# Low halves of weights by an accumulating DMA, and small tasks in other slots, in a two-block kernel

## The chip, the cores and the metric

One core of a Trainium2 chip runs the whole program. The metric is the device time of one execution in microseconds, from start to end of the program on that core; lower is better. All data is float32, and the products must be close to those of float32.

## The reference

Two transformer-like blocks, one after the other, on 256 tokens with 2048 features.

```python
# first block
h = rms(x) ; proj = h @ w_in                       # 8 parts of 1024 columns
y_rec = hgrn2(q, f_fwd, f_bwd, i, gate)            # gated linear recurrence in both directions, 8 heads
y_conv = b * conv3(c * h_conv)                     # short convolution, width 3
x = x + concat(y_rec, y_conv) @ w_out
x = x + (silu(g) * u) @ w_down                     # g, u = rms(x) @ w_gate_up, 5632 each
x = rms(x)
# second block
sh1, sc1, gt1, sh2, sc2, gt2 = split(silu(c) @ w_ada + b_ada)
h = rms(x) * (1 + sc1) + sh1 ; proj = h @ w_in_2
y_a = latent attention with rope, 8 heads ; y_b = stick-breaking attention, 8 heads
x = x + gt1 * ((sig(gl_a) * (y_a @ w_mla) + sig(gl_b) * (y_b @ w_sb)) @ w_out_2)
h2 = rms(x) * (1 + sc2) + sh2
x = x + gt2 * ((silu(gate) * up) @ w_ffn_out)      # gate, up = h2 @ w_ffn_in, 5632 each
```

## The kernel before, in words

All weights are read once from HBM, in units of 512 rows by 512 columns (1 MB, `raw`, four buffers, loaded by SyncE at L2009). A unit is worked off in two chunks (`hf` 0 and 1) of 256 rows. TensorE has a fast form of float32 (fp32r) that keeps only the high bits, so each product is made of three: every operand is split into a high half, which fp32r holds exactly, and a low half, the rest. ScalarE makes the high half of a chunk (`whi`, L865, in `cast(c)`), VectorE the low half (`wlo = raw - whi`, L1257, in `low(c)`), and TensorE then adds high x high, low x high and high x low into one accumulator (L834 to L836, in `products(v)`). There are four such buffers (HL = 4). A chunk is 12 products of 512 columns (two feature tiles, two halves m of the tokens, three terms).

The order of the work is written out in advance by `Plan`. A visit is one chunk on TensorE; slot s of an engine's program is its small tasks (`side_work(s)`) followed, on TensorE, by the products of visit s. On ScalarE slot s then casts the chunk that is three visits ahead (AHEAD), as soon as its buffer is free, which is when the visit before s has ended; on VectorE the lows of slot s - 1 stand first in slot s, then the tiles of the `ada` product, which VectorE computes alone (L1684), then the small tasks. SyncE loads unit u as soon as the last chunk of unit u - 4 has its low half. GpSimd does only the 20 small powers (x to the -0.5, L1933).

A block is a set of 512 columns of one matrix; `block_side(b, t)` holds what each engine does in slot t after the block's last visit. The blocks that the change touches:

- `h` (L1341, VectorE): the convolution in four parts, t = 3 to 6, two per half of the tokens; its result is used by block `b` at t = 2, eight slots after `h` ends.
- `hgrn(g, u)`: the recurrence of head group g as tasks u, one per slot, from slot H0 on. u = 0 to 2: Qx and KC (L1607, L1610), the latter used by TensorE at u = 3 (L633). Levels follow. u = 29, 30: outputs `hout` on TensorE. u = 30, 31: their squares summed on VectorE (L1634), mean, then the power on GpSimd. u = 32: scaling (L1641), u = 33: times the gate (L1647). u = 34, 35: TensorE turns the result (L553 is every turn's line), ScalarE writes its high half (L879), and at u = 35, 36 VectorE its low half (L1271).
- `latent` (t = 3: turns and high halves; t = 4: low halves).
- `gate_tiles` (L1720 to L1728): four times from slot GT0 on, every second slot; in the next slot TensorE spreads them over partitions (L733, L734) and ScalarE copies them to `gtB`. `gated_add` (L1537, L1545) uses gtB at the end of each `out2` block.
- `boundary(w, k)`: the two norms between blocks (w = 0, 1). There the order is skewed: the last four chunks of the old block are visited for m = 0 (k = 0 to 3), then for m = 1 (k = 4 to 7), then the first four chunks of the new one for m = 0 (k = 8 to 11) and m = 1 (k = 12 to 15), each visit six products. VectorE at k = 4: `add(0)`, `scale(0)`, `y0(0)` (L1808); TensorE turns the normed rows in pieces p (`norm_first(w, 0, p)`, amid the visits k = 6 to 9); ScalarE scales and shifts a turned piece (`shifted`, L1195), for p = 2 VectorE does it (L1846); VectorE splits it into halves (`piece`, L1815, L1817), which the visits from k = 8 on need; then the same for m = 1 (`add(1)` is L1528 and L1530 at w = 0).
- The start: 26 warm-up products (WARM, L841) before the first real one.

In the second ffn (blocks `fgate`, `fup` with arg (2, j)) the columns are done in two parts, j = 0 to 5 and 6 to 10, each followed by its four `fdown` blocks. At the end of each fgate block ScalarE does two sigmoids (L933) ahead of its cast. Units of `w_ada` are woven in; the last of them comes before the second part.

Of the kernel before, what the change touches and what calls it, by code (L numbers as in the profile page):

```python
# [28 lines left out]
WARM = 26  # L29
# [82 lines left out]
class Plan:  # L112


    def __init__(self, rows):
        self.blocks = plan_blocks()
        self.at = {(b.kind,) + b.arg: b for b in self.blocks}
        self.units, self.chunks, self.ada_unit = [], [], {}
        todo = [(j, g) for j in range(24) for g in range(4)]
        since = -4  # L120
        every_of = {"out": 4, "fgate": 2, "fup": 2, "fdown": 2}
        for b in self.blocks:
            if b.kind == "fgate" and b.arg == (2, 0):
                since = -4
            ng = rows[b.name] // NBLOCKS[b.name]
            for gi, g in enumerate(b.groups):
                u = len(self.units)
                self.units.append((b.name, b.nb * ng + g))
                for hf in range(1 if b.kind == "kpe" else 2):
                    self.chunks.append((b, 2 * gi + hf, u, hf))  # L130
                since += 1
                every = 4 if b.lhs == "h1" else every_of.get(b.kind)
                if b.kind == "fdown" and b.arg in ((1, 1, 2), (1, 1, 3)):
                    every = None
                late = b.kind[0] == "f" and b.arg[0] == 2
# [151 lines left out]
def two_block_kernel(nc, a, out):  # L287
    ctx = ExitStack()
    with ctx:
# [158 lines left out]

        def raw_here(u):
# [5 lines left out]
        sem_side = [sem(f"s_side{i}") for i in range(4)]  # L455
        sem_raw = [sem(f"s_raw{i}") for i in range(RAW)]
# [64 lines left out]
        GT0 = {2: pl.end("sb", 3) + 2, 5: pl.ada_done[23] + 2}  # L521
# [29 lines left out]
        def tensor_program(e):  # L551
# [18 lines left out]
            def block_side(b, t):  # L570
# [22 lines left out]
                elif kind == "latent" and t == 3:  # L593
# [25 lines left out]
            def hgrn(g, u):  # L619
# [34 lines left out]
                elif u in (34, 35):  # L654
                    p2 = u - 34
# [43 lines left out]
            def side_work(s):  # L699
# [103 lines left out]
            def products(v):  # L803
# [3 lines left out]
                if ms[0] == 0:  # L807
                    e.wait_ge(*on("dve_lo", c, 0))
# [39 lines left out]
        def scalar_program(e):  # L848
            def cast(c):
# [15 lines left out]
                e.copy(whi[i][:, :, :], raw[u % RAW][:, 2 * hf:2 * hf + 2, :]).then_inc(*ev("act_hi", c, 0))  # L865
# [16 lines left out]
            def block_side(b, t):  # L882
# [84 lines left out]
                elif kind == "latent" and t == 3:  # L967
# [76 lines left out]
            def hgrn(g, u):  # L1044
# [21 lines left out]
                elif u in (34, 35):  # L1066
                    scaled_high(mH, ("hturn", g, u - 34), 4 * g + 2 * (u - 34), "hgrn_norm_w")
# [97 lines left out]
            def boundary(w, k):  # L1165
# [42 lines left out]
                elif k == 7:  # L1208
                    shifted((0, 0), AUX[0], 0, P)
                    shifted((0, 1), AUX[1], 2, P)  # L1210
                elif k == 8:
                    squares(1)
                    shifted((0, 3), AUX[3], 6, P)
# [30 lines left out]
        def vector_program(e):  # L1244
            def low(c):
# [3 lines left out]
                if c == 0:  # L1249
                    for k in range(2):  # L1250
# [3 lines left out]
                        feature(1 + k)  # L1254
                    return
# [55 lines left out]
            def block_side(b, t):  # L1311
# [29 lines left out]
                elif kind == "h" and 3 <= t < 7:  # L1341
                    g, m, half = b.arg[0], (t - 3) // 2, (t - 3) % 2
# [94 lines left out]
                elif kind == "latent" and t == 4:  # L1437
# [161 lines left out]
            def hgrn(g, u):  # L1599
                lev = hlev(u) if u >= 6 else None  # L1600
                if u in (0, 1):
                    if u == 0:
# [3 lines left out]
                        e.wait_ge(*on("dve_gates", g, 0, 5))  # L1606
                    e.tensor_tensor(Qx[:, u, :], qT[:, :], TA[:, 1024 * u:1024 * u + 1024], ALU.mult).then_inc(  # L1607
                        *ev("dve_hgrn", g, "q", u))
                elif u == 2:
                    e.tensor_tensor(KC[:, :], Kx[:, 0, :], Kx[:, 1, :], ALU.add).then_inc(*ev("dve_hgrn", g, "kc"))  # L1610
# [20 lines left out]
                elif u in (30, 31):  # L1631
# [3 lines left out]
                    if m:  # L1635
                        e.wait_ge(*on("dve_hgrn", g, "ss", 1))
                        mean(("hgrn", g), b_o[g], 8, P)
                elif u == 32:
                    e.wait_ge(*on("pool_pow", "hgrn", g))
                    for m in range(2):  # L1640
                        e.tensor_tensor(v4(T[m]), v4(side("hout", g, m)),  # L1641
# [7 lines left out]
                elif u in (35, 36):  # L1649
                    scaled_low(mH, mL, ("hturn", g, u - 35), 4 * g + 2 * (u - 35), "hgrn_norm_w")  # L1650
# [126 lines left out]
            def boundary(w, k):  # L1777
# [62 lines left out]
                elif k == 8:  # L1840
                    add(1)
# [7 lines left out]
                    piece(0, 2)  # L1849
                    scale(1)  # L1850
                    piece(0, 3)
# [77 lines left out]
        def gpsimd_program(e):  # L1929
# [7 lines left out]
            for g in range(2):  # L1937
                power(b_s[g], b_o[g], 8, "hgrn", g)
# [12 lines left out]
            for m in range(2):  # L1951
                power(b_r5 + m, b_r5 + m, 1, "norm", 1, m)


        def sync_program(e):
# [34 lines left out]
            for u, (name, k) in enumerate(pl.units):  # L1990
# [10 lines left out]
                if u >= RAW:  # L2001
# [3 lines left out]
                    else:  # L2005
                        e.wait_ge(*on("dve_lo", pl.last_chunk[u - RAW], 0))
# [124 lines left out]
```

## Time and profile before

| what | value |
|---|---|
| median of 2 runs | 2611.93 us (2611.53 to 2612.33) |
| the profiled execution | 2611.4 us |
| its span, first to last instruction | 2609.6 us |
| granted TensorE clock, mean | 0.998 |
| read from HBM | 578.36 MB, 222 GB/s over the span |

Times in rows are microseconds from the span's start unless marked ns. PE is TensorE's products, PEld its weight loads, DVE VectorE, ACT ScalarE, POOL GpSimd, SP SyncE. L12 is line 12 of the kernel before. Matmuls are pipelined: a record of 0.39 us is followed by the next start 0.23 us later. A releaser (<-) is what ended an idle time.

### The profile page before, as it was taken

The page shows a single profiled execution, that of the slowest core. Times are in us where ns is not written, and L with a number is a line of the kernel's source. Part 1 is how long each engine was busy: PE and PEld are TensorE (multiplying, and loading weights), DVE is VectorE, ACT ScalarE, POOL GpSimd, SP SyncE. Part 2 cuts the span into 40 slices and gives each one's busy share as a digit, 9 for nine tenths or more (in the row PEclk, how much of TensorE's full clock was granted, in tenths as well). Part 3 has the DMA queues.
Part 4 walks back from the last instruction along what each step waited for, and adds up shares of the span by engine and source line. Part 5 has one row for each costly group of instructions (what it writes and reads, how often), then busy time and mean ns, then how long its engine had stood idle before and what let it go on. Part 6 is the DMA issues. An engine that isn't in the chain of part 4 may idle for free.

```text
span 2609.6 us, 29547 instructions
## 1 busy us (share of the span) xinstructions
PE 2591.0 (99%) x11900; PEld 2152.0 (82%) x11900; DVE 1757.9 (67%) x2156; ACT 1198.8 (46%) x1465; POOL 26.4 (1%) x25
## 2 busy tenths in 40 slices
PE   9999999999999999999999999999999999999999
PEld 8887887888888888888788888888788888888887
DVE  6777687787777778886565455466677755555554
ACT  6444544444443344445655454444544443344443
POOL 0000000000000000000000000000000000000000
PEclk9999999999999999999999999999999999999999
DMA  8655656688788887776455445555477755555554
GB/s 323 220 191 201 221 194 220 239 298 288 276 290 288 289 285 281 282 285 234 156 173 175 145 162 180 193 190 179 163 280 283 274 177 194 193 193 194 179 193 144
DMA packets 82632, 582.37 MB, mean 223 GB/s; under 512 B 9409, under 2 KB 9793, under 8 KB 12609
## 3 DMA queue, kind: packets, MB, share of 16 engines
q1 hardware_dynamic: 82352, 580.38, 63.3%
q8 instruction: 94, 1.54, 0.2%
q14 instruction: 42, 0.34, 0.0%
q10 hardware_dynamic: 144, 0.12, 0.0%
HBM read 578.36 MB, written 2.10 MB: 222 GB/s over the span
## 4 chain that ended last, share of the span: by engine, by line
PE 96%; DVE 3%; ACT 1%; issue 1%; DMA 0%; POOL 0%; ACTq 0%; DVEq 0%
PE bank L834 30%; PE bank L836 30%; PE bank L835 30%; PE bank L553 2%; PE bank L633 1%; DVE wlo L1257 1%; DVE adacc L1684 0%; PE bank L671 0%; PE bank L682 0%; PE bank L683 0%; ACT whi L865 0%; DVE Qx L1607 0%; DVE tmp L1355 0%; PE bank L652 0%; PE bank L641 0%
## 5 line engine op out<-in xcount | busy, mean ns | idle before, releaser
L1257 DVE TENSOR_TENSOR wlo<-raw,whi 128x1024 fp32r<-128x1024 f32 x886 | 1082.0, 1223 | 740.2 <-ACT whi L865 731.7
L865 ACT CAST whi<-raw 128x1024 fp32r<-128x1024 f32 x886 | 932.9, 1054 | 1017.4 <-PE bank L836 1007.3
L834 PE MATMUL bank<-whi,hH 128*128 128x512 f32 x2528 | 997.8, 395 | 0.5 <-DVE wlo L1252 0.5
L836 PE MATMUL bank<-whi,hL 128*128 128x512 f32 x2528 | 985.9, 390 | 0.0
L835 PE MATMUL bank<-wlo,hH 128*128 128x512 f32 x2528 | 985.0, 390 | 0.0
L836 PEld LDWEIGHTS bank<-whi,hL 128*128 128x128 f32 x2528 | 474.9, 188 | 99.9
L834 PEld LDWEIGHTS bank<-whi,hH 128*128 128x128 f32 x2528 | 475.5, 188 | 97.3 <-issue 0.9
L835 PEld LDWEIGHTS bank<-wlo,hH 128*128 128x128 f32 x2528 | 475.7, 188 | 95.9
L834 PE MATMUL bank<-whi,aH 128*128 128x512 f32 x704 | 274.5, 390 | 0.0
L1684 DVE SCALAR_TENSOR_TENSOR adacc<-raw,stat,adacc 128x512 f32<-128x512 f32 x360 | 269.6, 749 | 6.8
L836 PE MATMUL bank<-whi,aL 128*128 128x512 f32 x704 | 274.0, 389 | 0.0
L835 PE MATMUL bank<-wlo,aH 128*128 128x512 f32 x704 | 273.9, 389 | 0.0
L834 PEld LDWEIGHTS bank<-whi,aH 128*128 128x128 f32 x704 | 132.1, 188 | 27.3
L835 PEld LDWEIGHTS bank<-wlo,aH 128*128 128x128 f32 x704 | 132.2, 188 | 27.3
L836 PEld LDWEIGHTS bank<-whi,aL 128*128 128x128 f32 x704 | 132.1, 188 | 27.3
L553 PE MATMUL bank<-ident,tmp 128*128 128x128 f32 x530 | 75.0, 274 | 8.1 <-DVE tmp L1647 6.5
L553 PEld LDWEIGHTS bank<-ident,tmp 128*128 128x128 f32 x530 | 63.4, 141 | 23.6 <-DVE tmp L1647 7.3
L834 PE MATMUL bank<-whi,mH 128*128 128x512 f32 x128 | 51.3, 401 | 0.0
L836 PE MATMUL bank<-whi,mL 128*128 128x512 f32 x128 | 50.7, 396 | 0.0
L835 PE MATMUL bank<-wlo,mH 128*128 128x512 f32 x128 | 50.4, 394 | 0.0
L940 ACT CAST aH<-bank 128x512 fp32r<-128x512 f32 x44 | 23.6, 590 | 45.6 <-PE bank L553 45.6
L1933 POOL TENSOR_TENSOR stat<-stat 128x4 f32<-128x4 f32 (+3 forms) x20 | 24.4, 1231 | 1834.0 <-DVE stat L1277 1073.6
(295 smaller groups left out, 1421.8 us busy)
## 6 DMA issues: line engine op xcount, KB each, us to landing
raw<-in_w_gu_dram SPq DMA_DIRECT2D x176, 1024.0 KB, 4.9
raw<-in_w_ada_dram SPq DMA_DIRECT2D x96, 1024.0 KB, 4.8
raw<-in_w_down_dram SPq DMA_DIRECT2D x88, 1024.0 KB, 4.8
raw<-in_w_in_dram SPq DMA_DIRECT2D x62, 1024.0 KB, 4.8
raw<-in_w_in2b_dram SPq DMA_DIRECT2D x56, 1024.0 KB, 4.8
raw<-in_w_out_dram SPq DMA_DIRECT2D x32, 1024.0 KB, 4.8
raw<-in_w_in2a_dram SPq DMA_DIRECT2D x8, 1024.0 KB, 5.0
raw<-in_w_mla_dram SPq DMA_DIRECT2D x8, 1024.0 KB, 4.8
```

What stands on the lines that cost most here:

```text
L553: return e.transpose(o, i, ident[0:n, 0:n])
L633: ins = e.matmul(o[:, P * hd:P * hd + P], KC[:, base:base + P], qq, start=True, stop=True)
L834: e.matmul(o, xh[:, kt, sl], wh[:, i, :], start=k == 0, stop=False)
L835: e.matmul(o, xh[:, kt, sl], wl[:, i, :], start=False, stop=False)
L836: ins = e.matmul(o, xl[:, kt, sl], wh[:, i, :], start=False, stop=k == n - 1)
L865: e.copy(whi[i][:, :, :], raw[u % RAW][:, 2 * hf:2 * hf + 2, :]).then_inc(*ev("act_hi", c, 0))
L940: e.copy(aH[:, k0:k0 + 4, P * m:P * m + P], v4(side(b.index, m))).then_inc(*ev("act_half", b.index, m))
L1257: e.tensor_tensor(wlo[i][:, :, :], raw[u % RAW][:, 2 * hf:2 * hf + 2, :], f(whi[i][:, :, :]), ALU.subtract).then_inc(*ev("dve_lo", c, 0))
L1684: ins = e.scalar_tensor_tensor(d, src, col, d, ALU.mult, ALU.add)
L1933: e.tensor_tensor(sc(o, n), sc(i, n), sc(b_half, n), ALU.pow).then_inc(*ev("pool_pow", *key))
```

## The change

Ten edits.

1. `pl.added`: of the blocks fgate and fup (2, j) with j >= 6, every second unit, those whose last chunk is number 3 or 7 of its block (so chunks 2, 3, 6 and 7 of each of the ten blocks). For their chunks VectorE makes no low half. ScalarE writes, after the high half, minus the raw data rounded to fp32r (which is minus the high half) into `wlo`, and GpSimd issues a DMA that adds the raw data, read again from HBM, onto it. TensorE waits for that DMA (`added_low`), and SyncE's next load into the raw buffer waits for the negative copy instead of the low half.
2. WARM 26 to 30.
3. GT0 of part 2 one slot later.
4. `latent` turns and high halves at t = 4, low halves at t = 5.
5. hgrn's turns at u = 35, 36 and their low halves at 36, 37.
6. hgrn's KC at u = 0, the two Qx at u = 1 and 2.
7. hgrn's mean and power for each half m by itself.
8. The convolution at t = 3, 4 (first half of the tokens) and 8, 9 (second).
9. `norm_first(w, 0, p)`: p = 0, 1 before the visit k = 7, p = 2, 3 amid it, in place of one in each of k = 6 to 9.
10. At k = 7 ScalarE also shifts p = 3, and VectorE does its share of p = 2 and all four pieces; at k = 8 add(1), scale(1), y0(1) follow.

```diff
+        self.added = {u for u, c in self.last_chunk.items()
+                      if self.chunks[c][0].kind in ("fgate", "fup") and self.chunks[c][0].arg[0] == 2
+                      and self.chunks[c][0].arg[1] >= 6 and self.chunks[c][1] in (3, 7)}
...
-        GT0 = {2: pl.end("sb", 3) + 2, 5: pl.ada_done[23] + 2}
+        GT0 = {2: pl.end("sb", 3) + 3, 5: pl.ada_done[23] + 2}
...
-                elif u in (34, 35):
-                    p2 = u - 34
+                elif u in (35, 36):
+                    p2 = u - 35
...
+                for w, v0 in enumerate(SK):
+                    if s == v0 + 7:
+                        norm_first(w, 0, 0)
+                        norm_first(w, 0, 1)
...
-                    if 6 <= k <= 9:
-                        norm_first(w, 0, k - 6)
+                    if k == 7:
+                        norm_first(w, 0, 2)
+                        norm_first(w, 0, 3)
...
-                    e.wait_ge(*on("dve_lo", c, 0))
+                    e.wait_ge(*(added_low(c) if u in pl.added else on("dve_lo", c, 0)))
...
-                e.copy(whi[i][:, :, :], raw[u % RAW][:, 2 * hf:2 * hf + 2, :]).then_inc(*ev("act_hi", c, 0))
+                src = raw[u % RAW][:, 2 * hf:2 * hf + 2, :]
+                e.copy(whi[i][:, :, :], src).then_inc(*ev("act_hi", c, 0))
+                if u in pl.added:
+                    e.activation(wlo[i][:, :, :], src, ACT.Copy, bias=0.0, scale=-1.0).then_inc(*ev("act_neg", c))
...
+                if u in pl.added:
                     return
...
-                elif kind == "h" and 3 <= t < 7:
-                    g, m, half = b.arg[0], (t - 3) // 2, (t - 3) % 2
+                elif kind == "h" and t in (3, 4, 8, 9):
+                    g, m, half = b.arg[0], int(t >= 8), (t - 3) % 5
...
+            for c in added_chunks:
+                b, ci, u, hf = pl.chunks[c]
+                name, k = pl.units[u]
+                e.wait_ge(*on("act_neg", c))
+                e.dma_start(wlo[pl.buf[c]][:, :, :].rearrange("p a b -> p (a b)"),
+                            a[name][k][:, 1024 * hf:1024 * hf + 1024], accum_op=ALU.add).then_inc(
+                    sem_add[pl.buf[c] % HL], 16)
...
-                        e.wait_ge(*on("dve_lo", pl.last_chunk[u - RAW], 0))
+                        if u - RAW in pl.added:
+                            e.wait_ge(*on("act_neg", pl.last_chunk[u - RAW]))
+                        else:
+                            e.wait_ge(*on("dve_lo", pl.last_chunk[u - RAW], 0))
```

## Rows read from the trace of the kernel before

**Rows 1.** The page: busy time, share of the span, instructions.

```profile
PE 2591.0 (99%) x11900; PEld 2152.0 (82%) x11900; DVE 1757.9 (67%) x2156; ACT 1198.8 (46%) x1465; POOL 26.4 (1%) x25
```

**Rows 2.** Waits of TensorE, whole span: us in total, times, longest.

```profile
PE bank L553 <- DVE tmp L1647: 6.5, 2, 3.2
PE bank L834 <- DVE hL L1817: 1.7, 2, 0.8
PE bank L733 <- DVE tmpr L1728: 1.6, 1, 1.6
...
PE bank L553 <- DVE tmp L1808: 1.1, 2, 0.7
...
PE bank L633 <- DVE KC L1610: 0.4, 2, 0.2
```

**Rows 3.** Windows: PE, PEld, DVE, ACT, POOL busy; clock, DMA share, GB/s.

```profile
211.70:215.10 3.40, 2.71 (x9) 2.33 (x10) 1.77 (x3) 1.55 (x3) 0.00 (x0) 0.50 0.86 280
...
1803.00:1806.00 3.00, 1.40 (x7) 0.83 (x6) 2.96 (x6) 0.87 (x3) 0.00 (x0) 1.00 0.00 0
```

**Rows 4.** Timeline, 202 to 213: start, us, engine, line, [idle before].

```profile
202.45 0.47 DVE L1352 TENSOR_SCALAR tmp<-U,vec 128x128 f32<-128x128 f32 x2
202.84 1.13 DVE L1355 SCALAR_TENSOR_TENSOR tmp<-U,vec,tmp 128x128 f32<-128x128 f32 x4
...
211.05 1.28 DVE L1647 TENSOR_TENSOR tmp<-tmp,Gg 128x512 f32<-128x512 f32 x2
...
204.86 2.56 POOL L1933 TENSOR_TENSOR stat<-stat 128x8 f32<-128x8 f32 x1 [157.50 <-DVE stat L1277]
...
212.39 1.12 PE L553 MATMUL bank<-ident,tmp 128*128 128x128 f32 x4 [3.24 <-DVE tmp L1647]
```

**Rows 5.** Timeline of VectorE: the gated add ahead of the fourth gate tiles.

```profile
1800.80 0.69 DVE L1537 TENSOR_TENSOR tmp<-bank,gtB 128x512 f32<-128x512 f32 x1
```

**Rows 6.** Timeline of the first norm boundary: VectorE, then one turn on TensorE.

```profile
1242.50 0.29 DVE L1815 CAST hH<-aux 128x256 fp32r<-128x256 f32 x1 [1.37 <-ACT aux L1195]
1242.83 0.43 DVE L1817 TENSOR_TENSOR hL<-aux,hH 128x256 fp32r<-128x256 f32 x1
...
1244.78 0.68 DVE L1528 TENSOR_TENSOR tmp<-x,bank 128x512 f32<-128x512 f32 x1
...
1246.11 0.72 DVE L1846 TENSOR_SCALAR adacc<-bank,stat,adaF 128x128 f32<-128x128 f32 x2
...
1248.76 0.48 DVE L1808 TENSOR_SCALAR tmp<-x,stat 128x512 f32<-128x512 f32 x1
...
1249.91 0.38 PE L553 MATMUL bank<-ident,tmp 128*128 128x128 f32 x2
```

**Rows 7.** The start: timeline of TensorE, then a window (columns as in rows 3).

```profile
1.08 5.81 PE L841 MATMUL bank<-ones_r 128*128 128x128 f32 x26 [1.08 <-DVE ones_r L1908]
...
7.44 0.80 PE L834 MATMUL bank<-whi,hH 128*128 128x512 f32 x1 [0.55 <-DVE wlo L1252]
...
7.50:10.20 2.70, 2.70 (x7) 2.14 (x8) 2.52 (x5) 2.64 (x6) 0.00 (x0) 1.00 0.98 301
```

**Rows 8.** Timeline in the second part: ScalarE's casts, one product of TensorE.

```profile
2386.42 1.05 ACT L865 CAST whi<-raw 128x1024 fp32r<-128x1024 f32 x1
2388.17 1.05 ACT L865 CAST whi<-raw 128x1024 fp32r<-128x1024 f32 x1 [0.70 <-PE bank L836]
2390.89 1.05 ACT L865 CAST whi<-raw 128x1024 fp32r<-128x1024 f32 x1 [1.67 <-PE bank L836]
...
2387.97 0.39 PE L834 MATMUL bank<-whi,hH 128*128 128x512 f32 x1
```

**Rows 9.** Windows of that part (columns as in rows 3); landing of L2009's loads.

```profile
2275.00:2497.00 222.00, 222.00 (x997) 184.10 (x996) 116.90 (x112) 93.87 (x99) 0.00 (x0) 1.00 0.56 191
...
2389.70:2393.10 3.40, 3.40 (x17) 2.81 (x16) 1.91 (x2) 1.05 (x1) 0.00 (x0) 1.00 0.91 308
...
DMA to landing us min/median/max: 4.6/4.8/6.2
```

More of the change, by code:

```diff
@@ L28 @@
 SPARE = 4
-WARM = 26
+WARM = 30
 LIFE = 14
@@ L447, in side_read, with added_low @@
             return sem_side[n % 4], n // 4 + 1
+        def added_low(c):
+            return sem_add[pl.buf[c] % HL], 16 * sum(1 for d in added_chunks if d <= c and pl.buf[d] == pl.buf[c])
         def raw_here(u):
@@ L455, in two_block_kernel @@
         sem_side = [sem(f"s_side{i}") for i in range(4)]
+        sem_add = [sem(f"s_add{i}") for i in range(HL)]
+        added_chunks = [c for c, ch in enumerate(pl.chunks) if ch[2] in pl.added]
         sem_raw = [sem(f"s_raw{i}") for i in range(RAW)]
@@ L592, in block_side @@
                         ins.then_inc(*ev("pe_turn", b.index, m))
-                elif kind == "latent" and t == 3:
+                elif kind == "latent" and t == 4:
                     for p2 in range(2):
@@ L966, in block_side @@
                             *ev("act_lat", b.index, m))
-                elif kind == "latent" and t == 3:
+                elif kind == "latent" and t == 4:
                     for p2 in range(2):
@@ L1065, in hgrn @@
                         *ev("act_sq", "hout", g, m))
-                elif u in (34, 35):
-                    scaled_high(mH, ("hturn", g, u - 34), 4 * g + 2 * (u - 34), "hgrn_norm_w")
+                elif u in (35, 36):
+                    scaled_high(mH, ("hturn", g, u - 35), 4 * g + 2 * (u - 35), "hgrn_norm_w")
             def mla_head(h, t):
@@ L1210, in boundary @@
                     shifted((0, 1), AUX[1], 2, P)
+                    shifted((0, 3), AUX[3], 6, P)
                 elif k == 8:
                     squares(1)
-                    shifted((0, 3), AUX[3], 6, P)
                     y1(1)
@@ L1254, in low @@
                         feature(1 + k)
+                    return
+                if u in pl.added:
                     return
@@ L1436, in block_side @@
                         *ev("dve_mean", "latent", i))
-                elif kind == "latent" and t == 4:
+                elif kind == "latent" and t == 5:
                     i = b.arg[0]
@@ L1600, in hgrn @@
                 lev = hlev(u) if u >= 6 else None
-                if u in (0, 1):
-                    if u == 0:
+                if u == 0:
+                    e.wait_ge(*on("dve_gates", g, 0, 5))
+                    e.tensor_tensor(KC[:, :], Kx[:, 0, :], Kx[:, 1, :], ALU.add).then_inc(*ev("dve_hgrn", g, "kc"))
+                elif u in (1, 2):
+                    z = u - 1
+                    if z == 0:
                         q = pl.at["q", g].index
@@ L1605, in hgrn @@
                         e.wait_ge(*side_read(q, 1))
[L1606 to L1610, printed above, removed]
+                    e.tensor_tensor(Qx[:, z, :], qT[:, :], TA[:, 1024 * z:1024 * z + 1024], ALU.mult).then_inc(
+                        *ev("dve_hgrn", g, "q", z))
                 elif lev is not None:
@@ L1634, in hgrn @@
                     e.tensor_reduce(sc(b_o[g] + 4 * m, 4), v4(T[m]), AX_X, ALU.add).then_inc(*ev("dve_hgrn", g, "ss", m))
-                    if m:
-                        e.wait_ge(*on("dve_hgrn", g, "ss", 1))
-                        mean(("hgrn", g), b_o[g], 8, P)
+                    e.wait_ge(*on("dve_hgrn", g, "ss", m))
+                    mean(("hgrn", g, m), b_o[g] + 4 * m, 4, P)
                 elif u == 32:
-                    e.wait_ge(*on("pool_pow", "hgrn", g))
                     for m in range(2):
+                        e.wait_ge(*on("pool_pow", "hgrn", g, m))
                         e.tensor_tensor(v4(T[m]), v4(side("hout", g, m)),
@@ L1648, in hgrn @@
                             *ev("dve_hgrn", g, "gated", m))
-                elif u in (35, 36):
-                    scaled_low(mH, mL, ("hturn", g, u - 35), 4 * g + 2 * (u - 35), "hgrn_norm_w")
+                elif u in (36, 37):
+                    scaled_low(mH, mL, ("hturn", g, u - 36), 4 * g + 2 * (u - 36), "hgrn_norm_w")
             def carry(g, lev, t4, z, half, tz, name):
@@ L1839, in boundary @@
                     piece(0, 1)
-                elif k == 8:
-                    add(1)
                     o = side("norm", w, 0, 2)
@@ L1849, in boundary @@
                     piece(0, 2)
+                    piece(0, 3)
+                elif k == 8:
+                    add(1)
                     scale(1)
-                    piece(0, 3)
                     y0(1)
@@ L1937, in gpsimd_program @@
             for g in range(2):
-                power(b_s[g], b_o[g], 8, "hgrn", g)
+                for m in range(2):
+                    power(b_s[g] + 4 * m, b_o[g] + 4 * m, 4, "hgrn", g, m)
             power(b_r2, b_r2, 2, "r2")
```

## Prediction

> **What bounds the kernel now.** I read the page first: TensorE is busy for 2591.0 of 2609.6 us, 99% of the span, while VectorE has 67% and GpSimd 1% [rows 1]. So no other engine's work has a price of its own; only what TensorE waits for, or the rate at which it runs, can change. That leaves 18.6 us of idle time. The waits of TensorE by line come second [rows 2]: two waits of 3.2 us for the hgrn groups' gated values, 1.6 us for the first gate tiles, and 1.7 + 1.1 us for norm pieces and L1808 at the two norm boundaries. The rest is smaller waits, the start and the end. Third, the stretches around the two long waits by windows: the granted clock is 0.50, the lower of its two levels (1.2 instead of 2.4 GHz), for 3.4 us after a gap of 3.24 us (there are two such gaps, alike; the first is shown); around the gap of 1.6 us it stays at 1.00 [rows 3]. At half rate 3.4 us of busy time give 1.7 us of work, so each long gap costs 3.2 + 1.7 = 4.9 us.
>
> **The change, part by part.**
>
> *hgrn tail (tasks u = 30 to 37).* Before, TensorE reaches the turn of u = 34 when its products end, 3.24 us before it can start it at 212.39. VectorE is late: the convolution stands in slot 31 (202.45 to 203.97, 1.5 us) and again in slot 32 ahead of the sum of squares, and of the scaling L1641, and L1647 ends at 212.33 [rows 4]. The change takes both parts out of these slots (to t = 8, 9), splits the power by m, and puts the turn one slot later. Of the 3.0 us of convolution that go, the casts that wlo waits for, which TensorE's own pace sets, give back some; the 1.5 us of the second part I count as gained, so L1647 ends at about 210.8. The turn now comes at 209.15 + 2.72 = 211.9, where 2.72 us is the distance of two casts in steady work [rows 8]. So about 1 us is to spare, and the wait and the low clock both go: 2 x 4.9 = -9.8 us. Were nothing gained on VectorE, the moved slot alone would still cover 2.72 of the 3.24 us: -8.8 at least. Late next: the low halves of the second group, now at u = 36 and 37, are wanted in slots 38 and 39, so nothing waits. The moved convolution falls into slots 34 and 35, from which one L1271 pair has gone.
>
> *KC first.* TensorE waits 0.4 us in all for L1610 [rows 2]; KC moves ahead of two multiplications of the same size, so this goes: -0.4.
>
> *Gate tiles one slot later.* The last of four falls together with the gated add of out2 (0): four operations of 0.7 us from 1800.80 push L1728, and TensorE waits 1.6 us [rows 2, 5]. On odd slots they don't meet: -1.6. The copies to gtB move by one slot with them and are wanted four slots later.
>
> *Norm boundaries.* Four turns are now in slot 7 (two before, two amid), and VectorE does all four pieces before add(1). The first wait, for L1808, goes (1.1 in both), and so do those for the third piece. But add(1) starts later. At the first boundary it stands at 1244.78; now four pieces (0.29 + 0.43, thus 0.7 us each) and one L1846 pair (0.72) come before it from 1242.50 on, and ScalarE, at some 0.8 us a piece, holds the second by a little: 1246.15. From add(1) to the end of y0(1) it was 1244.78 to 1249.24, 4.5 us with a piece and an L1846 pair in between, and I count 4.1 without. So y0(1) ends at 1250.25, and the turn of m = 1 comes 0.3 us later than its 1249.91 [rows 6]; the same count at the second boundary gives 0.2. Together +0.5, with one gap of some 2 us per boundary in place of three short ones. Bounds: -2.8 (the waits of rows 2 there all gone) to +4 (0.5, and the clock lost twice at 1.7).
>
> *Start.* The warm-up products take 5.81 / 26 = 0.22 us each, so 30 end at 1.08 + 6.7 = 7.8 by the records, where the first real product began at 7.44; since each record is longer than its distance to the next, I take +0.2 of the 0.3. The seven starts of the next 2.7 us are at half rate, one in 0.39 us on average where steady work has 2.72 / 12 = 0.23, though the clock column says 1.00 [rows 7, 8]. If closing the gap brought the full rate at once, that would be 7 x 0.2 = -1.4.
>
> *Latent turns one slot later.* Nothing on TensorE waits for them, and the blocks that use them start slots later: 0, with a slot of cover.
>
> *The added low halves.* In the blocks fgate and fup j = 6 to 10 there are 40 chunks of the kind (ci 2, 3, 6, 7 in ten blocks), in the stretch 2275 to 2497, where TensorE never idles [rows 9]. VectorE loses 40 x 1.22 us and ScalarE gains 40 x 1.05 us; both are off the path there (117 and 94 us busy of 222), so neither pays or gains. The price is the landing. A cast starts 0.20 us after the first product of its slot (2387.97, 2388.17) [rows 8], and its chunk is multiplied three slots later: 8.16 - 0.20 = 7.96 us after the cast's start. Cast and negative copy, two in a row of 1.05 us with a slight overlap, end after 2.0 us. So 5.95 us are left from the signal to GpSimd until the data must have landed. After each of five fgate blocks ScalarE first does two sigmoids, and the cast is 0.97 us later: at 2386.42, where 2388.17 - 2.72 = 2385.45 was due [rows 8]; that cast is of ci = 3, an added one, which leaves 4.98 us.
>
> How long does the landing take? The trace has no accumulating DMA and none of GpSimd's. The nearest row is SyncE's load of 1 MB: 4.8 us to landing (4.6 to 6.2), of which 3.4 us are transfer with the engines 0.91 busy [rows 9]. Half the bytes alone: 4.8 - 1.7 = 3.1 us, the lower bound. Upper: the transfer takes twice its bytes (it reads the old values too) and shares the engines with a whole load, 4.8 - 3.4 + 3.4 + 3.4 = 8.2 us. The second chunk of each pair does meet a load, since the same act_neg event releases SyncE's next one; the first doesn't. I take the middle, 5.6 us: 15 pairs hide it, and in five TensorE waits 5.6 - 4.98 = 0.6 us, +3. Bounds: 0, and 15 x 2.25 + 5 x 3.22 = +50 us (once a pair waits, its second chunk has waited with it). In bandwidth: the engines are 0.56 busy there with 40 loads of 1 MB; 40 transfers of half a MB add 0.28 at the loads' time per byte, 0.84 in all, so there is room.
>
> **Sum.** -9.8 - 0.4 - 1.6 + 0.5 + 0.2 + 3 = -8.1 us, on the profiled execution's own 2611.4 (its span of 2609.6 and 1.8 around it): 2603.3. The median of the runs shown is 0.5 higher, so 2603.8.
>
> **Rivals.**
>
> *Late landings (slower).* One mechanism at one place: TensorE's wait at the added chunks. It decides from a landing of 6.3 us: 15 x (6.3 - 5.95) + 5 x (6.3 - 4.98) = 12 us is about what the rest saves (11.1). At 8.2 us it costs 50 us: 2611.9 - 11.1 + 50 = 2651. For it: a load beside every second one, and a SyncE load already took 6.2 us at worst. Against: the engines idle some 2 us in each unit's 5.4, and 5.95 us is more than the 1 MB load's 4.8.
>
> *The DMA engines are full (slower).* If an added transfer costs the time of twice its bytes, the share is 0.56 + 0.56 = 1.12, and the stretch of 222 us needs 249: +27, less some 12 us by which loads run ahead: 2616 at the least, 2628 at the most. Against: under pressure the engines may do better than the 308 GB/s of the row [rows 9].
> The Trainium skill (Collectives: The Full Stack, "The bandwidth ceiling: the fold count and why AG ≠ RS ≠ AR") says that an adding transfer is slow not for the sum but because it reads two sources, twice the traffic on the read side; no row here shows it yet. By it this rival would hold.
>
> *GpSimd or its queue falls behind (slower by over 2%).* GpSimd took 2.56 us for eight columns of a power [rows 4]; were its issue as slow as 3 to 4 us, or held up while VectorE works, landings of 9.5 us and more would make each pair wait 3.5 us and more and drop the clock as well (gap over 3.2 us, 1.7 each): 20 x (3.5 + 1.7) = 104 us, 2705. With the wait but no drop: 2671.
> The Trainium skill (SBUF — State Buffer, "SBUF: two separate sides") holds that GpSimd can't write the descriptors of its DMAs while VectorE runs an instruction that uses both of its ports. Here VectorE has no wlo in the added slots but has one in the others; no run yet shows a hold-up.
>
> *Boundaries lose the clock.* The 2 us gaps lie between the 1.6 that kept the clock and the 3.2 that lost it: +3.4, 2607.
>
> *All lands in time and the start gains.* 2611.9 - 11.1 - 1.4 = 2599.4.
>
> **How the numbers follow.** Forecast (adds hidden or nearly, 2599 to 2608 with the boundary and start cases inside): 0.50. Late landings, 2608 to 2664: 0.28, most of it under 2645. Engines full, 2616 to 2628: 0.09. GpSimd behind, over 2664: 0.13. The predicted time is 2603.8; the range 2597 to 2648 leaves out the last case, a bit of the second, and little below. Two per cent, 52 us, is about what a measurement of this kernel can tell from no change. All idle time and low clock together are some 40 us, so faster by that much is next to excluded: 0.01; slower 0.13; within 0.86.
>
> **What would show it.** In the profile after: no wait for L1647 and no clock of 0.50 near 212 and 420; none for KC or the gate tiles near 1805; at the boundaries one longer wait for L1808 in slot 11; at the 40 chunks the DMA of the POOL queue landing in 5 to 6 us, and TensorE waits only in five places. If TensorE's waits for the added DMA are twenty or more and over 1 us, the forecast is wrong at the landing; if the 3.2 us waits persist, at the hgrn step.

## The result, and the profile after

The median is 2665.62 us (2659.25 and 2672.0, two runs) beside 2611.93: 53.7 us slower, a ratio of 1.020 (95% interval 1.017 to 1.024). The profiled execution took 2659.25 us, its span is 2657.4. The forecast of 2603.8 and its whole range, up to 2648, are missed.

The page of the kernel after, in its parts on engines, DMA queues and DMA issues, answers to [rows 1]:

```profile
PE 2600.8 (98%) x11904; PEld 2155.5 (81%) x11904; DVE 1710.1 (64%) x2118; ACT 1235.5 (46%) x1505; POOL 62.4 (2%) x67
...
q1 hardware_dynamic: 82352, 580.38, 62.5%
q0 software_dynamic: 5760, 20.97, 4.3%
...
raw<-in_w_gu_dram SPq DMA_DIRECT2D x176, 1024.0 KB, 5.6
...
wlo<-in_w_gu_dram POOLq DMA_DIRECT2D x40, 512.0 KB, 7.8
```

VectorE is rid of 48 us of work, and the time has not gained by it. The last row is where the forecast breaks: the added transfers land 7.8 us after their issue in the median, where 5.6 had been taken. The queue rows tell more: q0, the adds, moved 20.97 MB for 4.3% of the engines' time, 0.205% per MB; q1, the loads, has 62.5 / 580.38 = 0.108% per MB. An added byte holds the DMA engines nearly twice as long as a loaded one.

The waits of TensorE after, which answer to [rows 2]:

```profile
PE bank L848 <- DMA wlo<-in_w_gu_dram: 46.4, 20, 3.5
PE bank L562 <- DVE tmp L1827: 2.8, 2, 1.6
PE bank L848 <- DVE hL L1836: 1.7, 2, 0.8
PE bank L855 <- DVE ones_r L1927: 1.1, 1, 1.1
PE bank L562 <- DVE tmp L1510: 0.6, 1, 0.6
```

The waits of the hgrn groups (6.5 us), the gate tiles (1.6) and KC (0.4) are gone. L1827 (L1808 before) has one longer wait at each norm boundary. Above them all stands a new one: 20 waits for the added low halves, one for each of the 20 pairs of chunks. Four of them in the timeline of TensorE (start, us, what, idle before):

```profile
2274.12 0.79 PE L848 MATMUL bank<-whi,hH 128*128 128x512 f32 x1 [3.52 <-DMA wlo<-in_w_gu_dram]
...
2305.88 0.50 PE L848 MATMUL bank<-whi,hH 128*128 128x512 f32 x1 [3.11 <-DMA wlo<-in_w_gu_dram]
2319.31 0.50 PE L848 MATMUL bank<-whi,hH 128*128 128x512 f32 x1 [2.25 <-DMA wlo<-in_w_gu_dram]
...
2375.41 0.50 PE L848 MATMUL bank<-whi,hH 128*128 128x512 f32 x1 [1.84 <-DMA wlo<-in_w_gu_dram]
```

The windows of the stretch with the adds answer to [rows 9]: first the whole, then three parts of the 8 us in which one second chunk of a pair travels. Columns are PE, PEld, DVE, ACT and POOL busy, clock, DMA share, GB/s.

```profile
2261.00:2545.00 284.00, 237.56 (x1003) 189.21 (x1003) 70.40 (x73) 131.09 (x139) 35.19 (x40) 0.97 0.87 225
...
2298.00:2301.00 3.00, 3.00 (x15) 2.48 (x14) 1.23 (x1) 1.45 (x2) 0.78 (x1) 1.00 0.84 216
2301.00:2303.00 2.00, 1.77 (x8) 1.13 (x6) 1.22 (x1) 0.34 (x2) 0.00 (x0) 1.00 0.97 252
2303.00:2305.00 2.00, 0.00 (x0) 0.00 (x0) 0.00 (x0) 1.81 (x2) 0.00 (x0) 1.00 1.07 227
```

TensorE never idled here before; now it does for 284.00 - 237.56 = 46.4 us, while the DMA engines' share has gone from 0.56 to 0.87. What happens in that second chunk's 8 us is read from the timeline around it (SPq is the issue of the next load, POOL that of the add) and from the DMA records:

```profile
2296.54 1.06 ACT L882 ACTIVATE wlo<-raw 128x1024 fp32r<-128x1024 f32 x1
2297.50 1.04 ACT L880 CAST whi<-raw 128x1024 fp32r<-128x1024 f32 x1
2297.63 0.33 SPq L2039 DMA_DIRECT2D raw<-in_w_gu_dram  x1
2297.90 0.88 POOL L1977 DMA_DIRECT2D wlo<-in_w_gu_dram  x1 [6.57 <-ACT wlo L882]
```

One event, the end of the negative copy L882, releases both. SyncE's issue is 0.27 us ahead. Counting the starts of the packets of each queue in steps of 0.5 us from the issue of an add gives, for this second chunk and for a first chunk issued at 2290.45, whose event releases no load (the row q1 shows the rest of the load issued 2.67 us before it):

```
second chunk (2297.90)  q1 load  0 16 1 8 26 20 24 16 13  4  0  0  0  5 13 28 ...
                        q0 add   0  0 0 0  0  0  0  0  7 12 29 24 25 24  7  0 ...
first chunk  (2290.45)  q1 load 30 25 20  2  0  0  0  0  0  0  0  0 ...
                        q0 add   0  0  0 16 20 16 24 24 23  4  1  0 ...
```

The load's 128 packets go first and the add's follow. The add's first packet starts 4.33 us after its issue, and it lands at 7.94; alone the first packet starts at 1.58 and it lands at 5.62. Over the 20 pairs the medians of the landing are 6.28 (first) and 7.96 us (second). It is only the second chunk of a pair that TensorE waits for.

### The profile page after: what moved, and what is told of

Read it like the earlier page. It is cut to its first block, busy times and chain, and to the rows that moved or that the text cites. A ratio compares the mean times of both kernels' runs of the same rounds, so it can differ in the third digit from the quotient of the medians.

```text
span 2657.4 us, 29599 instructions
## 1 busy us (share of the span) xinstructions
PE 2600.8 (98%) x11904; PEld 2155.5 (81%) x11904; DVE 1710.1 (64%) x2118; ACT 1235.5 (46%) x1505; POOL 62.4 (2%) x67
## 3 DMA queue, kind: packets, MB, share of 16 engines
q1 hardware_dynamic: 82352, 580.38, 62.5%
q0 software_dynamic: 5760, 20.97, 4.3%
## 4 chain that ended last, share of the span: by engine, by line
PE 91%; DMA 6%; ACT 1%; issue 1%; DVE 1%; POOL 0%; ACTq 0%; POOLq 0%
PE bank L848 29%; PE bank L850 28%; PE bank L849 28%; DMA wlo<-in_w_gu_dram 6%; PE bank L562 2%; PE bank L642 1%; ACT wlo L882 1%; PE bank L680 0%; PE bank L855 0%; PE bank L691 0%; PE bank L692 0%; ACT whi L880 0%; DVE wlo L1276 0%; DVE hL L1836 0%; PE bank L661 0%
## 5 line engine op out<-in xcount | busy, mean ns | idle before, releaser
L1276 DVE TENSOR_TENSOR wlo<-raw,whi 128x1024 fp32r<-128x1024 f32 x846 | 1033.6, 1223 | 780.6 <-ACT whi L880 772.9
L848 PE MATMUL bank<-whi,hH 128*128 128x512 f32 x2528 | 1002.8, 397 | 46.4 <-DMA wlo<-in_w_gu_dram 46.4
L1952 POOL TENSOR_TENSOR stat<-stat 128x4 f32<-128x4 f32 (+2 forms) x22 | 25.2, 1153 | 1821.9 <-DVE stat L1296 1060.9
L1977 POOL DMA_DIRECT2D wlo<-in_w_gu_dram x40 | 35.2, 880 | 636.3 <-ACT wlo L882 636.3
```

The source lines that it names most:

```text
L848: e.matmul(o, xh[:, kt, sl], wh[:, i, :], start=k == 0, stop=False)
L1276: e.tensor_tensor(wlo[i][:, :, :], raw[u % RAW][:, 2 * hf:2 * hf + 2, :], f(whi[i][:, :, :]), ALU.subtract).then_inc(*ev("dve_lo", c, 0))
L1952: e.tensor_tensor(sc(o, n), sc(i, n), sc(b_half, n), ALU.pow).then_inc(*ev("pool_pow", *key))
L1977: e.dma_start(wlo[pl.buf[c]][:, :, :].rearrange("p a b -> p (a b)"), a[name][k][:, 1024 * hf:1024 * hf + 1024], accum_op=ALU.add).then_inc ...
```

## The experiments

Kernels e1, e3 to e8 and e11 start from the kernel after; e2, e9 and e10 from the kernel before. Ratios are to the kernel before, with 95% intervals.

**The two halves of the change.** e1 has everything but the adds:

```diff
-        self.added = {u for u, c in self.last_chunk.items()
...
+        self.added = set()
```

> Edits 2 to 10 alone: no unit is in the added set, all low halves are VectorE's. If the whole loss sits at the added chunks (20 waits of TensorE for GpSimd's DMA, 46.4 us, and four stretches at the low clock there), this is faster than the kernel before by what the small tasks save: up to the first added chunk the changed kernel's profile is about 11 us ahead, so 2601 us (2599 to 2603), ratio 0.996. The rival, that the small tasks hurt too (the norm boundaries) and the adds cost less, wants 2606 or more.

Measured: 2600.31 us (2598.97 to 2601.14, four runs), ratio 0.9955 (0.9938 to 0.9971), 12.1 us under its own runs of before. It is the fastest kernel of the study and beats both given ones.

e2 has edit 1 alone on the kernel before.

> Edit 1 alone on the kernel before. If the parts simply add, this is 11 us slower than the changed kernel: 2670 to 2683, ratio 1.022 to 1.027, with 20 waits for the added DMA of 46 us in all and the two waits of 3.2 us for the hgrn groups back. If the small tasks shift the phase of the adds and so matter for them, the waits differ from 46 us by more than 5.

Measured: 2684.46 us (2680.9 to 2691.32, four runs), ratio 1.0279 (1.0262 to 1.0296), 1.5 us above the upper end expected. There are eight stretches at the lower clock in its part with the adds, where the kernel after has four, besides the two near 212 and 420. Its waits of TensorE:

```profile
PE bank L843 <- DMA wlo<-in_w_gu_dram: 49.3, 20, 5.8
PE bank L562 <- DVE tmp L1661: 6.5, 2, 3.2
```

The waits for the adds, 49.3 us, are within 5 us of the kernel after's 46.4, so the small tasks matter little for them. The small tasks save 12 us, and the adds cost 65 to 72 us. Most of the rest is about the adds.

**Which half of a pair?** e5 adds only the first chunk of each pair, e6 only the second. VectorE makes the low half of the other one.

```diff
-        self.added = {u for u, c in self.last_chunk.items()
...
+        self.added = {c for c, (b, ci, u, hf) in enumerate(self.chunks)
+                      if b.kind in ("fgate", "fup") and b.arg[0] == 2 and b.arg[1] >= 6 and ci in (2, 6)}
```

e6 has `(3, 7)` in place of `(2, 6)`. In both, the tests of edit 1 go by chunk and not by unit.

> The changed kernel with only the first chunk of each added pair (ci 2 and 6, 20 chunks) made by the adding DMA, the second by VectorE again. The load released with the second chunk is then not in front of any add; the load before it (2.7 us ahead) is nearly done when the add's packets come. Theory of the load in front: landings of 5.5 to 6 us against 5.95 to be had, TensorE waits 0 to 5 us in all, 2600 to 2606. Rival, every add costs by itself (GpSimd's issue, the adding, the engines' share): half of the 65 us that the adds cost in the changed kernel, about 2630.

> The mirror: only the second chunk (ci 3 and 7, 20 chunks), whose negative copy also releases SyncE's load 0.3 us before GpSimd issues. Theory of the load in front: first packet 4.3 us after the issue, landing 7.9 us, TensorE waits 20 times, 15 x 2.0 + 5 x 3.0 = 45 us and the clock in places, so nearly the whole loss with half the adds: 2645 to 2665. Rival, a cost for each add: about 2630, as with the first chunks.

Measured: e5 2603.51 us (2602.11 to 2607.36, five runs), ratio 0.9967 (0.9953 to 0.9981). e6 2661.96 us (2658.54 to 2675.12, four runs), ratio 1.0199 (1.0171 to 1.0226). The landings of the 20 adds, and e6's waits of TensorE; first e5:

```profile
DMA to landing us min/median/max: 5.3/5.6/5.8
```

then e6:

```profile
DMA to landing us min/median/max: 7.7/7.9/8.4
...
PE bank L847 <- DMA wlo<-in_w_gu_dram: 44.1, 20, 3.2
```

In e5 the view of the waits lists none for an add. (It leaves out those under 0.15 us. By the start of the same product, the nth one of 512 columns in either profile, e5 falls 2.2 us behind e1 in the part with the adds; another 0.7 us at the start and 1.5 us at a norm boundary have nothing to do with them.) With the same number of adds, bytes and GpSimd issues, one kernel loses 3 us on e1 and the other 62. What differs is the load that the same event releases. The first chunks of the change cost next to nothing by themselves.

**Take the load away from the add.** e3 makes the load wait for the landing of the add:

```diff
-                            e.wait_ge(*on("act_neg", pl.last_chunk[u - RAW]))
+                            e.wait_ge(*added_low(pl.last_chunk[u - RAW]))
```

> The changed kernel, but SyncE's load into an added unit's raw buffer waits for the landing of the add, not for the negative copy. Theory of the load in front: the second add of a pair starts its transfer 4.3 us after its issue because the load, released 0.3 us earlier by the same event, holds the engines; without it it starts at 1.6 us and lands in 5.5 to 6 us instead of 8. TensorE then waits under 1 us per pair, 0 to 12 us in all, and the time is 2601 to 2615. Rival, the adding transfer or GpSimd is slow by itself: landings of the second adds stay near 8 us, the time at 2655 to 2672. Second rival, the loads held back come late: TensorE or ScalarE waits for raw instead.

Measured: 2646.91 us (2643.75 to 2647.81, four runs), ratio 1.0130 (1.0115 to 1.0145), with 17 waits of 34.8 us in all. That is neither of the two times expected (up to 2615, or 2655 and more). The collision has moved, not gone. The held load and the one that follows in SyncE's order now go out 0.37 us apart, 2.6 and 3.0 us ahead of the next pair's first add, whose first packet then starts at 4.2 us. Landings are 7.75 us (first) and 7.46 (second) in the median; the two adds issued at 2342.89 and 2346.88, with no load issued from 5 us before the first until both had landed, took 5.5 us each.

e8 turns ScalarE's two operations round, so that the add is issued earlier and the load 0.67 us after it:

```diff
+                if u in pl.added:
+                    e.activation(wlo[i][:, :, :], src, ACT.Copy, bias=0.0, scale=-1.0).then_inc(*ev("act_neg", c))
                 e.copy(whi[i][:, :, :], src).then_inc(*ev("act_hi", c, 0))
-                if u in pl.added:
-                    e.activation(wlo[i][:, :, :], src, ACT.Copy, bias=0.0, scale=-1.0).then_inc(*ev("act_neg", c))
...
-                            e.wait_ge(*on("act_neg", pl.last_chunk[u - RAW]))
+                            e.wait_ge(*on("act_hi", pl.last_chunk[u - RAW], 0))
```

> The changed kernel with the negative copy ahead of the high half on ScalarE; SyncE's load waits for the high half, so it is issued some 0.7 us after GpSimd's DMA instead of 0.3 us before. The add has 0.95 us more until it is wanted. If landings stay at 8.0 us, each of the 20 waits shrinks by 0.95: about 19 us and some low clock saved, 2640 to 2650. If the order of the two issues decides which transfer goes first, the second adds land in 5.5 to 6.5 us and nearly all waits go: 2601 to 2615.

Measured: 2649.16 us (2643.88 to 2651.95, four runs), ratio 1.0138 (1.0123 to 1.0153), 20 waits of 31.7 us for the adds. Two more, of 4.1 us, are put down to ScalarE's high half by the view, but end 0.13 us after an add has landed (at 9.4 and 9.6 us), some 9 us after that high half was written: they are the adds' too, 35.8 us in all. The landing of the second chunk stays at 8.2 us in the median. Now the two transfers mix. The count of packet starts from the issue of such a chunk at 2318.99 is:

```
q1 load   0  0 0  0  0 10 5 10  9 14 16 15  9 10 24  6 ...
q0 add   23 14 1 16 10  5 0 16 16 13  6 13 16 16  1  0 ...
```

The first packets of q0 still belong to the pair's first add; this add's own start from 1.6 us on and are spread over 5.4 us, against 3.4 for the one alone shown above. It lands at 8.31 and its load at 8.48 us. So turning the order of the two issues round doesn't help. The 16 us by which e8 is under the kernel after are near the 19 that were expected of the earlier issue alone, a cast of 1 us no longer standing ahead of it.

e11 holds the load until VectorE has made the low half of the chunk after the pair, some 3 us after the add's issue:

```diff
                             e.wait_ge(*on("act_neg", pl.last_chunk[u - RAW]))
+                            e.wait_ge(*on("dve_lo", pl.last_chunk[u - RAW] + 1, 0))
```

> The changed kernel (40 adds in pairs) with SyncE's load into an added unit's buffer held until VectorE has the low half of the next chunk, about 3 us after the negative copy: its packets then come some 4 us after GpSimd's issue, when the add's are nearly through, and it is not bunched with the next load as it was when held until the landing. If all that is wrong is where the loads fall, the second adds land in 5.5 to 6.2 us and TensorE waits 0 to 5 us: 2600 to 2608. If the engines' time is short as well (per two units two loads of 2.5 to 3.4 us and two adds of 2.7 us against 10.9 us), adds are still late in places, as with the first chunk of every unit (13 us of waits, 2624): 2610 to 2630. Rival, the order doesn't matter: 2647 or more, as with the two other moves of the load.

Measured: 2621.23 us (2613.74 to 2622.29, eight runs), ratio 1.0029 (1.0019 to 1.0040). The first packet of a pair starts at 1.6 to 2.9 us, landings are 5.4 to 7.8 us, and the mean clock is 1.000. Of the 60 us by spans, 40 are saved by this one line. Waits of TensorE in e11, and a window of it (columns as before):

```profile
PE bank L848 <- DMA wlo<-in_w_gu_dram: 12.7, 16, 1.8
...
2262.00:2500.00 238.00, 225.21 (x979) 178.55 (x978) 67.99 (x70) 128.47 (x136) 34.63 (x40) 1.00 0.96 259
```

**What is left then?** e7 adds the first chunk of every unit: 40 adds again, evenly spread, none of them with the load of the same event.

```diff
-        self.added = {u for u, c in self.last_chunk.items()
...
+        self.added = {c for c, (b, ci, u, hf) in enumerate(self.chunks)
+                      if b.kind in ("fgate", "fup") and b.arg[0] == 2 and b.arg[1] >= 6 and hf == 0}
```

> As many adds as in the changed kernel (40) and the same bytes, but the first chunk of every unit instead of both of every second, so each add meets the load released 2.7 us before it and none is issued with one. If only the position against the load counts: landings of 5.5 to 6 us and 2600 to 2610. If the DMA engines' time counts (an add takes 0.328 us for 4 KB, as much per packet as the load's 8 KB: 2.6 us per add and 3.4 us per load against 5.4 us for a unit, 1.10 in all), loads fall back, adds land in 7 us and later, and the time is 2630 or more.

Measured: 2624.38 us (2619.38 to 2626.97, four runs), ratio 1.0043 (1.0028 to 1.0058), between the two times expected, 14 waits of 13.1 us with landings up to 8.3 us. The same window of e7:

```profile
2262.00:2500.00 238.00, 224.79 (x979) 178.65 (x978) 68.00 (x71) 128.08 (x135) 34.04 (x39) 1.00 0.95 262
```

The same of e5, half the adds:

```profile
2262.00:2500.00 238.00, 237.94 (x1062) 194.65 (x1061) 100.49 (x99) 118.24 (x126) 17.64 (x20) 1.00 0.78 232
```

And of e1, none:

```profile
2262.00:2500.00 238.00, 238.00 (x1072) 197.55 (x1071) 125.40 (x120) 100.41 (x106) 0.00 (x0) 1.00 0.55 189
```

With 20 adds and a share of 0.78 all land in time. With 40, in both placements that keep the load of the same event away (e7, e11), the engines are 0.95 to 0.96 busy and 13 us of waits remain. By q0's row of the kernel after, one add holds 16 engines for 0.043 x 2657.4 / 40 = 2.86 us; 40 take 114 us, and 0.55 x 238 = 131 us of loads make it 245 us of work in 238. For e5 the same count gives (57 + 131) / 238 = 0.79, and 0.78 is measured. That the last 13 us come of the engines' time is argued from this count. It isn't shown: no run has plain copies in the places of e7 or e11, which would tell.

**What does the adding itself cost?** e4 copies the raw data in place of adding them, with the same bytes read, order and queue. It leaves out the addition, so those low halves are the raw weights.

```diff
-                            a[name][k][:, 1024 * hf:1024 * hf + 1024], accum_op=ALU.add).then_inc(
+                            a[name][k][:, 1024 * hf:1024 * hf + 1024]).then_inc(
```

> The changed kernel with GpSimd's DMA as a plain copy onto the low half, without the addition (the low halves of the 40 chunks are then the raw weights; that part of the result is left wrong). If adding doubles the transfer, a packet of 4 KB takes about 0.16 us instead of 0.33, an unhindered landing is 1.3 us shorter (4.3 instead of 5.6), the second of a pair lands in 6.5 instead of 8, and TensorE waits 20 to 25 us instead of 46: 2630 to 2642. If the cost is GpSimd's issue and the queue behind the load alone, landings change by under 0.5 us and the time stays at 2655 or more.

Measured in one run: 2627.66 us beside 2612.39 of before. It came 2.3 us under the range expected. Its queue row, waits and landings:

```profile
q0 software_dynamic: 5760, 20.97, 2.2%
...
PE bank L848 <- DMA wlo<-in_w_gu_dram: 15.6, 12, 2.7
...
DMA to landing us min/median/max: 3.8/5.7/8.6
```

2.2% where adding has 4.3%: the median 4 KB packet takes 0.174 us copied and 0.328 us added. GpSimd's issue takes 0.54 us in place of 0.88, too. Landings are 4.0 us for first chunks and 5.86 for second ones. Even a plain copy behind the load is late in 12 places, with a third of the waiting time. So both are needed for the loss of 46 us: the place behind the load, and a transfer that takes nearly twice its time. (GpSimd's issue, 0.34 us shorter in e4, is a small part of it.)

**The hgrn step by its parts,** on the kernel before. e9 puts only the turn one slot later (edit 5), e10 only moves the convolution (edit 8).

> On the kernel before, only hgrn's turns and low halves one slot later. My step said this alone covers 2.72 of the 3.24 us: a wait of 0.5 us at each of two places, no clock lost, 2602 to 2604. Rival, the wait stays at some 3 us because VectorE is later still: 2611.

> On the kernel before, only the second half of the convolution moved to t = 8, 9. VectorE ends L1647 1.5 to 3.3 us earlier with the turn where it was, so the wait falls from 3.2 to between 0 and 1.7 us, twice, and no clock is lost: 2601 to 2606. Rival, the casts hold VectorE anyway and the wait stays over 2 us: 2608 to 2611.

Measured in one run each, beside 2612.64 of before: 2604.63 us and 2603.59 us. The waits of TensorE for L1647, first e9, then e10:

```profile
PE bank L553 <- DVE tmp L1647: 1.0, 2, 0.5
```

```profile
PE bank L553 <- DVE tmp L1647: 1.1, 2, 0.5
```

Either part alone cures most of it, and neither has a stretch at the lower clock near 212 or 420. By the start of the same product before and behind the two hgrn groups, e9 and e10 gain 8.3 us each and the kernel after 9.8. The two do not add up: together they only remove the last 0.5 us of wait per group. The 1.0 us between the two runs is their start, not hgrn: at 30 us e9 is already 1.0 us behind e10.

## Why the prediction was wrong

By its own steps, against the spans: 2657.4 (after) and 2597.2 (e1), 60.2 us for the adds.

*The step that failed is the landing of the added low halves.* The text took "the middle, 5.6 us", let 15 pairs hide it and five wait 0.6 us: +3. Measured are 6.28 us for the first and 7.96 us for the second chunk of a pair, and it is the second that decides. (The text had it that the first of a pair waits and the second has waited with it; it is the other way round.) Put 7.96 into the prediction's own formula: 15 x (7.96 - 5.95) + 5 x (7.96 - 4.98) = 45 us; 46.4 are measured. The times available were nearly right: landing less wait is 4.8 us at the five sigmoid places, where 4.98 was counted (waits of 3.0 to 3.2 us, 2305.88 is one), and 5.8 to 6.7 at the other fifteen, where 5.95 was. The upper bound, 8.2 us and +50, was right, and so was its mechanism: twice the bytes' time, beside a whole load. The lower bound, 3.1 us, was not: the shortest landing of an add is 5.3 us (e5), and of a plain copy 3.8 (e4). What was wrong is taking the middle between bounds of which the upper one had been derived from something that the text itself said happens in every pair, "the same act_neg event releases SyncE's next one". 5.6 us happens to be right for the first chunks alone (e5), by luck, as the middle of a bound that was too low and one for another case. The rival of late landings, 0.28, was what came true, though the time of 2665.6 lies just above the 2608 to 2664 it was given, for the clock below.

*The clock was left out of that term.* In the profile after it stands at the lower level for 3.4 us at four of the 20 waits, from 0.7 us before the end of the first and 0.4 to 1.4 us after the end of the others (windows, columns PE busy, clock, DMA share, GB/s):

```profile
2273.40:2276.80 3.40, 2.68 (x6) 0.50 1.06 306
2290.50:2293.90 3.40, 3.40 (x9) 0.50 1.01 267
2306.00:2309.40 3.40, 3.40 (x15) 1.00 1.04 293
2362.20:2365.60 3.40, 3.40 (x9) 0.51 0.92 181
2375.80:2379.20 3.40, 3.40 (x10) 0.50 1.00 264
```

The third window is one that kept the full rate. The first goes on for another 3.4 us. TensorE is busy for 16.3 of the 17 us at the lower level, at half rate, so 8.1 us are lost. TensorE is busy 2600.8 us where e1 has 2587.1, 13.7 more. So 46.5 us of the 60.2 are idle time and 8.1 the clock. The remaining 5.6 stand around the 20 waits: the idle time counts from the end of a record, 0.39 us after its start, where the steady pace is 0.23, which leaves out 0.16 us each time (3.2), and after each wait the first product is followed by the next 0.33 us later instead of 0.23 (some 2). The other execution after, at 2672.0, had a lower mean clock (0.992 against 0.996); 0.004 of 2660 is 11 us, which is most of the 12.8 between the two. The range's upper end of 2648 counted no clock in the late case, and missed for it as well.

*Twice the bytes' time.* The trace showed none of it before; e4 and the queue rows now do (0.328 against 0.174 us a packet). The Trainium skill (Collectives: The Full Stack, "The bandwidth ceiling: the fold count and why AG ≠ RS ≠ AR") gives the reason as two sources to read; the trace agrees with the size, 1.9, though no run shows the reason.

*The rival of full engines* was priced at 2616 to 2628. It isn't what makes the change slow, since e11 with the same transfers saves 40 us. But it is what remains once the collision is gone: e7 and e11 measure 2624.4 and 2621.2. Its objection, that the engines might do better under pressure, did not hold: a loaded MB takes 2.86 us of the 16 engines after (0.625 x 2657.4 / 580.38) and took 2.85 before.

*GpSimd behind* fell: its issue takes 0.88 us in all 40 but the first (1.06). Whether a busy VectorE holds it up was hardly tested: VectorE runs something during only seven of the forty, the first among them, and the other six take 0.88 us like the rest.

*hgrn, -9.8:* right. By the start of the same product, after gains 9.8 us on before across the two groups. L1666 (L1647 before) ends at 209.03, 1.8 us earlier than the text had it, and the turn is at 211.30 with no wait:

```profile
211.30 0.60 PE L562 MATMUL bank<-ident,tmp 128*128 128x128 f32 x4
```

e9 shows that the moved slot alone leaves a wait of 0.5 us per group, as counted (3.24 - 2.72), and saves 8.3 us where at least 8.8 was said. What the text undervalued is the convolution, which alone would have done as much (e10: L1647 ends at 210.07).

*KC -0.4 and gate tiles -1.6:* their waits are gone, and by the start of the same product they bring somewhat more, 1.0 and 1.9 us.

*Norm boundaries, +0.5:* one longer wait each, 1.6 and 1.3 us, where some 2 was said; the two of 0.8 us for L1836 (L1817 before) are still there. By the start of the same product the first boundary takes 0.1 us more than before and the second 0.1 less: 0.0. No clock was lost there in the profile after:

```profile
1239.26 0.66 PE L562 MATMUL bank<-ident,tmp 128*128 128x128 f32 x4 [1.55 <-DVE tmp L1827]
```

That is not safe. In e4 a wait of 1.52 us at the same place was followed by 3.4 us at the lower clock (from 1242.8), and in e5 one of 1.25 us at the second boundary (from 1866.0). The rival that the boundaries lose the clock holds in single executions, at one boundary and for half its 3.4 us.

*Start, +0.2:* near enough, 0.1 in the profile after. The first real product starts at 7.55 us instead of 7.44, and the full rate comes at 10.37 instead of 10.32; closing the gap brings nothing. The "clock column says 1.00" of the text is no reading: the record of the clock only begins at 10.32 us, where the half rate ends, and a window ahead of it shows 1.00 for want of a record. In the 13 traces the half rate ends anywhere from 9.7 (e3) to 13.1 us (e9), which shifts a single profile by up to 1.6 us whatever the kernel.

Together the small tasks were to bring 11.1 us and brought 12.1 (e1, medians) or 12.4 (spans).

*A sum beside the forecast.* "All idle time and low clock together are some 40 us" is too much. By the text's own rows they are 18.6 + 2 x 1.7 = 22 us, and 23 with the start. A gain of 52 us was even further away than said.

## What to carry to other kernels

When a change puts a transfer on the path, look for what the same event releases on the other queues, and cost the transfer behind that; where the worst case is one that happens every time, take its value and not the middle between it and the best. An accumulating DMA is to be counted at twice its bytes against the engines' free time, and if the sum comes near 1 half the work can be free (e5) and the whole not (e7). A slack that is exceeded by 1.2 to 3.5 us, twenty times, can cost the clock on top of the waits (four times here, 8.1 us).

## What was not expected of the hardware

- Two transfers from different queues are not shared evenly. With the load issued 0.27 us ahead of the add, all the load's packets start first; with the load 0.67 us behind (e8) they mix and both end late. The Trainium skill (DMA: Bandwidth & Descriptors, "Queues, rings and completion order") has each engine drain a whole packet, a bundle of several descriptors, of one queue before it turns to the next; the 8 records that a load has per engine all going first agrees with it, the mixing in e8 is not explained by it alone.
- The length of a wait doesn't decide by itself whether the clock falls: after 3.11 us at 2305.88 it stayed at 1.00, after 1.84 us at 2375.41 it fell to 0.50 (windows above). At the first norm boundary it fell after 1.52 us in e4 and stayed after 1.55 us in the kernel after; at the second it fell after 1.25 us in e5 and stayed after 1.26 us. In e11 the longest wait was 1.85 us and none lost it. What decides was not tried.
- GpSimd's issue of an adding DMA takes longer than that of a plain one of the same shape, 0.88 against 0.54 us (e4).
